# Start addresses of the on-chip buffers in a two-layer encoder kernel: matmul operands at multiples of 1,024 or 2,048 bytes, the others at multiples of 64

## The reference

```python
for layer in range(2):
    if layer % 2 == 0:
        x = x + even_mixer(rmsnorm(x, a0_norm), a0_w_in, a0_w_out, a0_rpb)
    else:
        x = x + odd_mixer(rmsnorm(x, a1_norm), a1_w_qkv, a1_w_out, ...)
    g, wg, wu, wd = ffn_params[layer]
    h = rmsnorm(x, g)
    x = x + (silu(h @ wg) * (h @ wu)) @ wd
return rmsnorm(x, final_norm)
```

## Time and profile before

| | |
|---|---|
| Time, median of 3 runs | 2679.14 us (2676.55 to 2681.08) |
| Span of the profiled execution | 2678.1 us, clock 0.991 |
| TensorE matmul busy | 2645.2 us, 99% |
| TensorE weight loads busy | 2158.6 us, 81% |
| DVE busy | 1776.4 us, 66% |
| ACT busy | 1115.7 us, 42% |
| POOL busy | 141.8 us, 5% |

### The profile page before, as it was taken

One profiled execution on the slowest core, in us unless ns is written; L12 is line 12 of the kernel. 1 busy time (PEld: TensorE's weight loads), 2 busy tenths in 40 slices (PEclk: granted clock), 3 DMA queues, 4 the chain that ended last, 5 costly groups with the idle time before them and its releaser, 6 DMA issues.

```text
span 2678.1 us, 37390 instructions
## 1 busy us (share of the span) xinstructions
PE 2645.2 (99%) x13531; PEld 2158.6 (81%) x13531; DVE 1776.4 (66%) x2918; ACT 1115.7 (42%) x1998; POOL 141.8 (5%) x142
## 2 busy tenths in 40 slices
PE   8999999899999999999999999999999999999998
PEld 6888788788888888888878888888888888888887
DVE  5566665655766666666777777777556666666666
ACT  5555555534333222323455555555343233223233
POOL 0001022400000000000000000000000000000001
PEclk9999999999999999999999999998999999999999
DMA  3223243421111111111311111112211111111112
GB/s 122 58 59 83 67 121 110 146 106 51 52 48 55 52 59 47 47 52 56 116 45 47 47 47 47 47 47 100 68 52 55 48 48 56 51 55 50 47 47 83
DMA packets 101725, 173.75 MB, mean 65 GB/s; under 512 B 27296, under 2 KB 36944, under 8 KB 100048
## 3 DMA queue, kind: packets, MB, share of 16 engines
q1 hardware_dynamic: 90560, 162.26, 19.4%
q10 hardware_dynamic: 11024, 9.60, 1.4%
HBM read 151.74 MB, written 20.08 MB: 64 GB/s over the span
## 4 chain that ended last, share of the span: by engine, by line
PE 93%; DVE 2%; ACT 2%; issue 1%; SPq 1%; DMA 1%; POOL 0%; ACTq 0%; POOLq 0%; DVEq 0%
PE PS L2064 19%; PE PS L2066 19%; PE PS L2065 19%; PE PS L2144 18%; PE PS L2225 5%; PE PS L2294 5%; PE PS L2250 3%; PE PS L2241 1%; PE PS L2210 1%; PE PS L2271 1%; PE PS L2157 1%; PE PS L2071 1%; PE PS L2275 1%; SPq L513 0%; PE PS L2200 0%
## 5 line engine op out<-in xcount | busy, mean ns | idle before, releaser
L2144 PE MATMUL PS<-HH,WS 128*128 128x512 f32 x1536 | 516.7, 403 | 9.7 <-DVE HL L1402 8.5
L1179 ACT ACTIVATE WS<-WR 128x512 fp32r<-128x512 f32 x254 | 159.3, 629 | 443.3 <-PE PS L2066 321.5
L2144 PEld LDWEIGHTS PS<-HH,WS 128*128 128x128 f32 x1536 | 285.9, 189 | 67.3 <-DVE WS L1408 8.3
L2144 PE MATMUL PS<-HL,WS 128*128 128x512 f32 x768 | 302.4, 394 | 0.0
L1860 DVE TENSOR_TENSOR X<-PS,X 128x512 f32<-128x512 f32 x352 | 232.8, 685 | 76.3 <-PE PS L2066 74.4
L2064 PE MATMUL PS<-AH,WS 128*128 128x512 f32 x704 | 280.2, 398 | 0.0
L2066 PE MATMUL PS<-AH,WS 128*128 128x512 f32 x704 | 278.8, 396 | 0.0
L2065 PE MATMUL PS<-AL,WS 128*128 128x512 f32 x704 | 278.5, 396 | 0.0
L2064 PE MATMUL PS<-TH,WS 128*128 128x512 f32 x640 | 251.5, 393 | 0.0
L2066 PE MATMUL PS<-TH,WS 128*128 128x512 f32 x640 | 250.0, 391 | 0.0
L2065 PE MATMUL PS<-TL,WS 128*128 128x512 f32 x640 | 248.8, 389 | 0.0
(11 more groups left out here) (251 smaller groups left out, 4574.8 us busy)
## 6 DMA issues: line engine op xcount, KB each, us to landing
WR<-wstrips SPq DMA_DIRECT2D x304, 256.0 KB, 2.7
DR<-wdown SPq DMA_DIRECT2D x88, 256.0 KB, 2.6
BIASC<-ali_c SPq DMA_DIRECT2D x8, 960.0 KB, 6.9
BIAS<-tab_b SPq DMA_DIRECT2D x4, 1536.0 KB, 8.8
Y<-y_scratch SPq DMA_DIRECT2D x12, 512.0 KB, 6.3
BIAS<-ali_a SPq DMA_DIRECT2D x4, 1152.0 KB, 7.1
ya_scratch<-YS ACTq DMA_DIRECT2D x32, 128.0 KB, 2.4
MA<-a_scratch SPq DMA_DIRECT2D x16, 256.0 KB, 4.7
```

The costliest lines, as they stand in the source:

```text
L1179: e.activation(WS[:, slot, 0, :], src, ACT.Copy).then_inc(S["w_hi"], 1)
L2144: last = e.matmul(ps, wt, xt, start=g == 0, stop=g == 23)
```

## The change

Every buffer keeps its size, its type and its users; only start addresses change. Thirteen small buffers are placed first, everything after them starts at 18,432 (nine times 2,048), the rounding becomes 64 bytes, and the feed-forward's buffers behind `X` start at the next multiple of 1,024. Each engine executes the same instructions in the same order with the same waits as before.

```diff
     def sb(name, shape, dt=f32):
         size = int(np.prod(shape[1:])) * 4
         t = nc.alloc_sbuf_tensor_at(name, shape, dt, offset=place[0])
-        place[0] += -(-size // 32) * 32
+        place[0] += -(-size // 64) * 64
         return t
+
+    ONES = sb("ONES", [128, 8])
+    GAIN = sb("GAIN", [128, 5, KC])
+    SUBG = sb("SUBG", [128, 2])
+    NEGLAM = sb("NEGLAM", [128, 4])
+    EPS = sb("EPS", [128, 2])
+    RT = sb("RT", [128, KC, NQ])
+    LS = sb("LS", [128, 2, 2, NQ])
...
+    CE = sb("CE", [128, 2, 2 * NQ])
+    assert place[0] <= 18432
+    place[0] = 18432
 
     products_at = place[0]
     HH = sb("HH", [128, KC, T], f32r)
@@ -98,20 +114,7 @@
     WS = sb("WS", [128, 4, 2, 512], f32r)
     WR = sb("WR", [128, 2, 512])
     IDENT = sb("IDENT", [128, 128])
-    ONES = sb("ONES", [128, 8])
-    GAIN = sb("GAIN", [128, 5, KC])
...
     ST = sb("ST", [128, 2, 8])
-    LS = sb("LS", [128, 2, 2, NQ])
...
@@ -168,7 +171,7 @@
     place[0] = after_x
     LV = sb("LV", [128, 4, DH])
     LP = sb("LP", [128, 2, DH])
-    place[0] = after_x
+    place[0] = -(-after_x // 1024) * 1024
     AH = sb("AH", [128, 2, T], f32r)
```

More of the change, by code:

```diff
@@ L90, in sb @@
         t = nc.alloc_sbuf_tensor_at(name, shape, dt, offset=place[0])
-        place[0] += -(-size // 32) * 32
+        place[0] += -(-size // 64) * 64
         return t
+    ONES = sb("ONES", [128, 8])
[5 more added lines that the diff above has]
+    LS = sb("LS", [128, 2, 2, NQ])
+    LR = sb("LR", [128, 2, 2, NQ])
+    L0 = sb("L0", [128, KC, NQ])
+    EL = sb("EL", [128, KC, NQ])
+    CN = sb("CN", [128, 2, 2, NQ])
+    CD = sb("CD", [128, 2, 2 * NQ])
+    CE = sb("CE", [128, 2, 2 * NQ])
+    assert place[0] <= 18432
+    place[0] = 18432
     products_at = place[0]
@@ L100, in build @@
     IDENT = sb("IDENT", [128, 128])
-    ONES = sb("ONES", [128, 8])
-    GAIN = sb("GAIN", [128, 5, KC])
[L103 to L106, removed]
-    ST = sb("ST", [128, 2, 8])
-    LS = sb("LS", [128, 2, 2, NQ])
[L109 to L114, removed]
+    ST = sb("ST", [128, 2, 8])
     CW = sb("CW", [128, 2, 2 * NQ])
```

## The result

The change made the kernel faster: 2652.9 us median against 2678.8 us (four runs each, measured side by side), a ratio of 0.9903 with a 95% interval of 0.9891 to 0.9915. That is 25.9 us, where 2642 us (37 less) was forecast in a range of 2570 to 2672. The profiled execution took 2651.4 us with a span of 2649.6; so some 1.8 us lie around a span, which I had taken as nothing for the kernel before. From span to span it is 28.5 us. Of these, 2.3 us lie at matmuls that ran at half clock in one of the two profiled executions: half clock was granted for 49.7 us of the span before and for 45.8 after. The rest, 26, agrees with the medians.

A forecast was written before the change was run, and what follows sets the result against it. TensorE, busy 99%, bounds the kernel: number of matmuls times their pace. 26.2 + 3.7 + 4.0 + 1.6 + 2.6 - 1 = 37.1 us saved gives a median of 2642 us, range 2570 to 2672 (own case 2627 to 2655).

The forecast's parts named there:

- the pace of `TH` as the goal for `AH` and `FH`: Feed-forward: 3,936 matmuls on `AH`, `AL`, `FH`, `FL` go from 233.3 to 226.7 ns each, saving 26.2 us.
- The slow starts after `AH` and `FH`: Feed-forward: 100 turns to `TH` after these operands each lose a slow start of 0.037 us, saving 3.7 us.
- The cause: Moving operands: a row starting 32 past a multiple of 64 touches one more 64-byte piece, costing 6.67 ns per matmul.
- distance to the weights: Rival, 0.10: only operands at the same place modulo 2,048 as `WS` run at 226.7; feed-forward gains nothing, 2671 us.
- The attention: Attention: 4.0 us saved on `ATC`, `ATB`, `ATA`, 1.6 on scores, 2.6 on the projection's slow starts; 8.2 in all.
- 1 given back for waits: Attention: evictions and exponentials don't get faster, so 1 us of the 8.2 saved returns as waits.
- `HH`, `TH` and `WS` at 0: Projections and `three`: moving from 128 past to 0 past a multiple of 1,024 gains 0 on 4,992 matmuls.
- the boundary at 1,024: Rival, 0.17: crossing a 1,024-byte boundary costs 6.67 ns, so 8,928 matmuls save 59.6 us more, 2582 us.
- the full cost beside the columns: Rival, 0.08: all 13.3 ns beyond the columns go on 8,928 matmuls, 119 us, giving 2523 us.
- The slower rival: Rival, 0.05: weights and moving operands at the same place in every 1,024 bytes collide; +33, 2712 us less some gain.
- The rule on 16-byte cachelines: SBUF: rows starting 32 or 64 past touch 128 lines alike, so by it alone the change is worth nothing.
- DVE, ACT, the waits: Other engines: an address costs DVE and ACT 5 ns at most, taken as 0; feed-forward DVE goes from 66% to 68%.

The follow-up runs named there:

- Experiment 1: The kernel before with sizes rounded up to 64 bytes instead of 32, nothing moved to multiples of 1,024: 2677.99 us against 2677.67, ratio 1.0003.
- 6: The changed kernel with everything from `HH` on, the feed-forward's buffers too, 32 bytes later, distances to `WS` kept: 2652.59 us, ratio 0.9906 to the kernel before.
- experiment 4: The changed kernel with layer 1's attention buffers behind `FS` at multiples of 1,024 instead of 128 past one: 2653.26 us, ratio 0.9909 to the kernel before.
- Experiment 11: The changed kernel with down products moving only the first 384 of each 512 columns (output not the reference's): one run, 2551.59 us.
- experiment 5: The changed kernel with only the weights buffer `WS` (and `WR`) 32 bytes later: 2699.61 us, ratio 1.0084 to the kernel before.
- experiment 12: The kernel before with one pad of 224 bytes ahead of `region`, so `AH` and `FH` lie 0 from `WS` modulo 256: 2652.04 us, ratio 0.9895.
- experiments 2: The changed kernel with the feed-forward's buffers (`AH` to `FL`) 32 bytes later: 2678.19 us, ratio 1.0004 to the kernel before.
- 8: The changed kernel with `AH`, `AL` 64 and `FH`, `FL` 512 bytes past a multiple of 1,024: 2663.89 us, ratio 0.9945 to the kernel before.

## Why the prediction was right, and where it was not

*What bounds the kernel, and the pace of `TH` as the goal for `AH` and `FH`: right.* 226.7 ns on all of them, forecast 26.2 us, measured 13.7 + 10.8 = 24.5 from start to start. Of the 1.7 that are missing, about 1 us are waits between these matmuls that grew: one on `FH` early in the first feed-forward, which wasn't there before,

```profile
PE PS L2067 <- DVE SIL L1857: 0.5, 1, 0.5
```

and the two ahead of the transposes of `RT`, by 0.5 us together.

*The slow starts after `AH` and `FH`: right.* Forecast 3.7, measured 3.7. The hundred turns cost 36.7 ns each before and nothing now.

*The cause: wrong.* The step that failed is the one from 6.67 ns to "one piece of 64 bytes", which made the offset by 32 the cause. The number fits, and so does distance 32; the trace of before held one slow and one fast case, and both theories told them apart. Experiment 1 put the offset right and left the pace slow, 6 put all offsets wrong and had it fast. The rival "distance to the weights" was the right idea with the wrong period: it had 2,048 and therefore gave the feed-forward nothing, while 1,024 apart is 0 modulo 256. So the total came out by luck as far as the reason goes: the change removed the offset of 32 and, without my aiming at it, also made the distance 0 modulo 256. The kernel that does only what the stated reason asks for, number 1, gained nothing.

*The attention: wrong, 8.2 us forecast and nothing to be seen.* All three terms (4.0 on `ATC`, `ATB` and `ATA`, 1.6 on scores, 2.6 on slow starts) came from the false cause. By distance nothing could change, as those distances were 0 before. These 8.2, less the 1 given back for waits, are most of the 37.1 - 28.5 = 8.6 by which the sum was too large; the 1.7 above make up the rest. With the attention's terms at nothing the prediction's sum gave 29.9 us, or 2649. Its own range around these ends should read 2628 to 2654, not 2627 to 2655; 2652.9 lies in both, near the slow end. The slow starts of the projection are still there: its matmuls at the full clock, starts over 260 ns apart left out, cost 5.3 us beyond 226.7 ns each in the kernel before and 5.5 now, and experiment 4 shows that where `EC` starts isn't their cause. Experiment 11 shows such starts at distance 0 after a change from 384 to 512 columns; in the attention, where 128, 256 or 512 columns of other operands run before the projection, that may be the reason too, but no run shows it there.

*`HH`, `TH` and `WS` at 0: right.* 226.7 before and after; neither the boundary at 1,024 nor the full cost beside the columns. The 215.7 ns of the Trainium skill ("TensorE: Matmul & The Clock Gate", section "Wait — 56ns, not 53.3ns?") is seen in no run.

*The slower rival was upside down.* It feared the same place for weights and moving operands. Being at the same place is what makes 512 columns fast, and experiment 5 shows the slow side: 22 us above the kernel before.

*The rule on 16-byte cachelines* (the Trainium skill, "SBUF — State Buffer", section "Specifications (TRN2)"), taken alone, made the offset by 32 worth nothing. I had held the trace against it. Experiments 1 and 6 agree with the rule: the offset was worth nothing.

*DVE, ACT, the waits: right.* 686 and 689 ns on DVE against the earlier trace rows, and no group of waits grew by more than 0.5 us.

## What to carry to other kernels

Where a weight load runs beside each matmul, look at the start of the moving operand less that of the weights, modulo 256 bytes. For 512 columns of `fp32r` 0 was best here; a matmul took 1% longer at 64 and 3% longer at the other multiples of 32. One pad may set it, as in experiment 12; rounding every buffer up isn't needed. And when two cases in a trace differ by an exact number, write down every property of the addresses that tells them apart before giving the number to one of them: a single kernel with one property changed would have decided it.

## What the runs showed of the hardware that was not expected

- The pace of a matmul on 512 columns depends on the distance between the two operands in SBUF with a period of 256 bytes: 226.7, 233.3, 229.0, 233.3, 233.3, 233.8, 233.3 and 233.3 ns at 0 to 224. Shifting one operand moves it (experiments 2 and 5), shifting both does not (6). At half clock it is 427 ns at distance 0 and 32 alike. That the two reads meet in the same part of SBUF is the likely mechanism; no run shows it directly, and none has matmuls of 512 columns at the full clock without a weight load beside them, which would show whether the load is needed for it.
- For 256 columns 0 is not the best distance: 120 ns at 0, some 117 at 32 and at 64. Others weren't tried.
- At distance 0 a matmul costs 13.3 ns beside its columns at the full clock, whether it has 256 (120 ns), 384 (173.3) or 512 (226.7).
- After a change of distance or of the number of columns the pace takes up to ten matmuls to settle, with starts from 224 to 242 ns apart on `TH`. One turn to `TH` costs 36.7 ns after distance 32 (before), 50 after distance 64 (8), and 41 after 384 columns at distance 0 (11).
